# Splitting the picks' dot products between VectorE and ScalarE in a two-block transformer kernel

## The chip, the cores and the metric

The kernel runs on one core of a Trainium2 chip. The core has TensorE (PE in the rows), VectorE (DVE), ScalarE (ACT), GpSimd (POOL) and SyncE (SP), each with its own queue that runs strictly in the order in which it was written, and 16 DMA engines that all queues share. Engines wait for each other through semaphores. The metric is device time in microseconds (us); the times of before are the median of 3 runs. Everything is float32.

## The reference, cut to what matters

Two blocks follow each other on 256 tokens of width 1024. The first one ends in a retrieval of single-neuron experts (PEER), and that is where the change lies. For each token and each of 8 heads it scores two times 128 keys, takes the 16 best of each, combines them into 256 candidates, and takes the 16 best of those: the picks. Each pick names one of 16384 rows of two tables:

```python
top_s, pos = lax.top_k(combo, PEER_TOPK)
expert = jnp.take_along_axis(ids, pos, axis=-1)
g = jax.nn.softmax(top_s, axis=-1).astype(hb.dtype)
u_sel = peer_u[expert]
a = jax.nn.gelu(jnp.einsum('bqhkd,bqd->bqhk', u_sel, hb))
v_sel = peer_v[expert]
return jnp.einsum('bqhk,bqhkd->bqd', g * a, v_sel)
```

The second block (two layers of windowed attention and gated mixing, with large projections) starts when the sum over all picks is done.

## The kernel before

The tokens are two tiles of 128, one token to a partition. Eight heads and two tiles make 16 rounds g = 0 to 15, called heads here; each has 16 picks, so there are 256 picks. One pick is one gather: for each of 128 tokens a row of `peer_uv`, 1024 numbers of u and 1024 of v, 1 MB in all. It lands in one of 12 slots (`pair(n)`, n modulo 12; the slots lie in the tiles `rows` and `low_pairs`).

All engines work in program order, written out by hand. Within a head the picks go in four groups of four (`groups_of`), called groups 0 to 3; the last head has groups of 4, 2, 2 and then eight of one.

- **GpSimd** issues the gathers (L908 in the profile, the call that starts at L908). For pick n it waits until TensorE has summed pick n - 12 (`pair_used`).
- **VectorE** does `dot` for each pick of a group: one fused multiply and sum, 1024 wide, of the u half with the token's vector `h2_tok` in PSUM (L2070; the accumulator is read by a second short instruction). Then `weigh` makes four weights (L2081), for which it waits for the GELU. Behind the groups 0, 1 and 2 of head g it does one step each of the routing of head g + 2: `route_halves`, `route_pairs`, `route_experts` (L2020 to L2057).
- **ScalarE** waits for the group's four dots (`dotted`), takes their GELU (L1146), waits for `weighted` and writes four diagonal matrices (L1152). Up to head 4 its queue holds two more things: between groups 1 and 2 `score_query` copies the next queries out of PSUM as soon as TensorE has made them (L1109), and between groups 2 and 3 `score_out` copies the key scores (L1115). At a head's end stands `gate_exps`, an exponential with its table load (L1129), behind which the table for GELU is loaded again.
- **TensorE** multiplies a pick's v half by its diagonal and adds into PSUM (`sum_pair`, L1576), eight matmuls a pick, each of which is two in the rows, so a group is x64. Up to head 4 `score_query` of head g + 3 (L1552) stands between groups 1 and 2 and `score_keys` (L1565) between groups 2 and 3.

The queries and scores of the last heads are thus made while the first five heads (0 to 4) are summed; from head 5 on the picks are alone but for small things (a transpose, `join`, two weight pieces of the next block). SyncE loads one 1 MB weight unit during the picks.

Of the kernel before, what the change touches and what calls it, by code (L numbers as in the profile page):

```python
# [14 lines left out]
ALU = mybir.AluOpType  # L15
ACT = mybir.ActivationFunctionType
# [8 lines left out]
NT = T // P  # L25
D = 1024
# [6 lines left out]
EXPERT_HEADS, KEYS, PICKS = 8, 128, 16  # L33
# [220 lines left out]
def groups_of(g):  # L254

    sizes = [GROUP] * (PICKS // GROUP)
    if g == NT * EXPERT_HEADS - 1:
        sizes = [GROUP, 2, 2] + [1] * SINGLES
    at, out = 0, []
    for size in sizes:  # L260
        out.append((at, size))
        at += size
    return out
# [6 lines left out]
LAST_GROUP = NT * EXPERT_HEADS - 1  # L270
# [47 lines left out]
def build(nc, a, out):  # L318
    ctx = ExitStack()
    with ctx:  # L320
# [3 lines left out]
        def sem(name):  # L324
            return ctx.enter_context(nc.semaphore(name))
# [103 lines left out]
        dots = [w3.take(PICKS) for _ in range(2)]  # L429
# [13 lines left out]
        def pair(n):  # L443

            k = n % SLOTS
            return rows[:, k, :] if k < PAIRS else low_pairs[:, k - PAIRS, :]
# [39 lines left out]
        h2_tok = [pj[:, :, :].rearrange("p b n -> p (b n)"), aux[:, 0:2, :].rearrange("p b n -> p (b n)")]  # L486
# [38 lines left out]
        def at(l, per, k):  # L525
# [10 lines left out]
        h2_turned = sem("h2_turned")  # L536
        routed, gate_exp, dotted, dots_act, weighted, diag_ready = (
            sem("routed"), sem("gate_exp"), sem("dotted"), sem("dots_act"), sem("weighted"), sem("diag_ready"))
        pair_loaded = [sem(f"pair_loaded{s}") for s in range(SLOTS)]
        pair_used = sem("pair_used")  # L540
        single_gates, single_diag = sem("single_gates"), sem("single_diag")
# [387 lines left out]
        def _(act):  # L929
# [212 lines left out]
            for g in range(NT * EXPERT_HEADS):  # L1142
                for k, (first, size) in enumerate(groups_of(g)):
                    some = slice(first, first + size)
                    act.wait_ge(dotted, g * PICKS + first + size)
                    nc.scalar.activation(act_dots[g % 2][:, some], dots[g % 2][:, some], ACT.Gelu_apprx_tanh).then_inc(dots_act, 1)  # L1146
                    if size > 1:
                        act.wait_ge(weighted, GROUPS_BEFORE[g] + k + 1)
                    for j in range(first, first + size if size > 1 else first):
                        if g:  # L1150
                            act.wait_ge(pair_used, (g - 1) * PICKS + j + 1)
                        nc.scalar.activation(diag[:, j, :], ident[:, :], ACT.Copy, scale=weight[g % 2][:, j:j + 1]).then_inc(diag_ready, 1)  # L1152
                    h = g + AHEAD + 1
                    if h < EXPERT_HEADS and k == 1:
                        score_query(h)
                    if h < EXPERT_HEADS and k == 2:
                        score_out(h)
                    if g == EARLY_GROUP and k < EARLY_PIECES:
                        layer_hi(act, 0, k)
                    if g == LAST_GROUP and first == 11:  # L1160
                        act.wait_ge(pair_used, XH_PICKS)
                        x0_hi(0)
                if g + AHEAD < NT * EXPERT_HEADS:
                    gate_exps(g + AHEAD)
# [592 lines left out]
        def _(dve):  # L1757
            v = nc.vector
# [306 lines left out]
            def dot(g, j):  # L2065

                n = g * PICKS + j
                dve.wait_ge(pair_loaded[n % SLOTS], 16 * (n // SLOTS + 1))
                row = pair(n)[:, 0:D]
                v.tensor_tensor_reduce(row, row, h2_tok[g // EXPERT_HEADS], 1.0, 0.0, ALU.mult, ALU.add,  # L2070
                                       dots[g % 2][:, j:j + 1]).then_inc(dotted, 1)

            def weigh(g, k, first, size):

                some = slice(first, first + size)
                dve.wait_ge(dots_act, GROUPS_BEFORE[g] + k + 1)
                if size == 1:
                    v.tensor_scalar(diag[:, first, :], ident[:, :], act_dots[g % 2][:, some], weight[g % 2][:, some], ALU.mult, ALU.mult) \
                        .then_inc(single_diag, 1)
                    return  # L2080
                v.scalar_tensor_tensor(weight[g % 2][:, some], act_dots[g % 2][:, some], gate_inv[g % EXPERTS], gate[g % EXPERTS][:, some],  # L2081
                                       ALU.mult, ALU.mult).then_inc(weighted, 1)
# [17 lines left out]
            for g in range(NT * EXPERT_HEADS):  # L2100
                t, nxt = g // EXPERT_HEADS, g + AHEAD
                if g % EXPERT_HEADS == 0:
                    dve.wait_ge(h2_turned, t + 1)
                dve.wait_ge(gate_exp, g + 1)
                chain.link(v.reciprocal(gate_inv[g % EXPERTS], gate_sum[g % EXPERTS]))
                for k, (first, size) in enumerate(groups_of(g)):
                    for j in range(first, first + size):
                        dot(g, j)
                    weigh(g, k, first, size)
                    if g == LAST_GROUP and first + size == PICKS - SINGLES:  # L2110
                        singles = slice(first + size, PICKS)
                        v.tensor_scalar(weight[g % 2][:, singles], gate[g % EXPERTS][:, singles], gate_inv[g % EXPERTS], None, ALU.mult) \
                            .then_inc(single_gates, 1)
                        dve.wait_ge(single_gates, 1)
                        dve.wait_ge(pair_used, (g - 1) * PICKS + PICKS)
                    if nxt < NT * EXPERT_HEADS:
                        if k == 0:
                            route_halves(nxt)
                        if k == 1:
                            route_pairs(nxt)  # L2120
                        if k == 2:
                            route_experts(nxt)
                    if g == EARLY_GROUP and k == 3:
                        layer_lo(dve, 0, *range(EARLY_PIECES))
                    if g == EARLY_GROUP + 1:
                        dve.wait_ge(bias_iota, 1)
                        for h in (2 * k, 2 * k + 1):
                            v.tensor_scalar(bias8[:, h, :], distance, -(2.0 ** -(h + 1)) / ATT_SCALE, None, ALU.mult).then_inc(bias_lin, 1)
                    if g == LAST_GROUP and first == 12:
                        dve.wait_ge(pair_used, XL_PICKS)  # L2130
                        x0_low(0)
                if g == EXPERT_HEADS + 1:
                    dve.wait_ge(pair_used, EXPERT_HEADS * PICKS)
                    join(0)
# [263 lines left out]
```

## Time and profile before

| | us |
|---|---|
| median of 3 runs | 1173.74 (1173.55 to 1173.74) |
| the profiled execution | 1174.32 |
| its span, first to last instruction | 1172.5 |
| TensorE busy | 1048.3 (89%) |
| VectorE busy | 838.1 (71%) |
| ScalarE busy | 429.7 (37%) |
| GpSimd busy | 269.9 (23%) |
| share of the chain of waits: PE, DMA, DVE, ACT | 62%, 25%, 7%, 4% |

Three stages can be told apart. Up to about 190 us the first block's projections and attention run. From 178 us (the first gather) to 833 us (the last dot) the picks are gathered, scored and summed. Behind that the second block runs to the end. The busy shares are means over all three and say little of any one of them; the windows of the picks have to be read on their own. A line's busy time counts the instruction alone, and the wait ahead of it is given as idle time with the engine and line that ended it.

### The profile page before, as it was taken

The numbers are of one execution on the slowest core, as the hardware profiler recorded it, in microseconds if no ns is written. First come the engines' busy times: TensorE is split into PE (matmuls) and PEld (weight loads), VectorE is DVE, ScalarE is ACT, GpSimd is POOL, SyncE is SP. The second block draws the span as 40 slices with busy tenths as digits, with TensorE's granted clock in tenths as the row PEclk, the third lists the DMA queues.
The fourth block names the chain that finished last, engine by engine and source line by source line (L and its number), as shares of the span: only waits on it lengthen the run. The fifth ranks groups of instructions, "written<-read, shape, count | busy, mean of one in ns | idle before, by whom it ended". The sixth has DMA issues, their size and how long they took to land.

```text
span 1172.5 us, 18875 instructions
## 1 busy us (share of the span) xinstructions
PE 1048.3 (89%) x7587; PEld 978.6 (83%) x7587; DVE 838.1 (71%) x1802; ACT 429.7 (37%) x905; POOL 269.9 (23%) x289
## 2 busy tenths in 40 slices
PE   7999997999999988777787778878999999999997
PEld 6999986998899887677787777778999888898885
DVE  6998987667567667666777766655665868775776
ACT  3636732123212221222132122211457554476452
POOL 2001004343334333333333333434000000300000
PEclk9999998999999999999899999989999999999999
DMA  9986858999999999999999999999865655455540
GB/s 370 407 329 226 349 191 330 420 421 421 420 421 420 421 420 421 420 421 421 420 421 420 420 421 422 420 421 420 340 221 176 229 202 180 158 202 180 194 165 36
DMA packets 59576, 390.35 MB, mean 333 GB/s; under 512 B 6881, under 2 KB 7905, under 8 KB 15714
## 3 DMA queue, kind: packets, MB, share of 16 engines
q0 software_dynamic: 36864, 268.45, 55.1%
q1 hardware_dynamic: 21152, 120.10, 27.6%
q8 instruction: 60, 0.98, 0.3%
q10 hardware_dynamic: 1474, 0.60, 0.2%
q14 instruction: 26, 0.21, 0.0%
HBM read 388.08 MB, written 1.05 MB: 332 GB/s over the span
## 4 chain that ended last, share of the span: by engine, by line
PE 62%; DMA 25%; DVE 7%; ACT 4%; issue 1%; SPq 0%; ACTq 0%; DVEq 0%
PE aux L1576 23%; DMA rows<-in_peer_uv,work 23%; PE pj L1619 6%; PE pj L1620 6%; PE pj L1621 6%; PE pj L1293 5%; PE pj L1295 5%; PE pj L1294 5%; PE aux L1552 4%; DVE rows L2070 2%; DVE rows L1767 1%; DMA rows<-in_w_ada 1%; ACT work L1152 1%; ACT rows L1019 1%; PE aux L1432 1%
## 5 line engine op out<-in xcount | busy, mean ns | idle before, releaser
L1576 PE MATMUL aux<-work,rows 128*128 128x128 f32 x2080 | 261.0, 289 | 73.7 <-ACT work L1152 73.7
L1576 PEld LDWEIGHTS aux<-work,rows 128*128 128x128 f32 x2080 | 253.8, 204 | 81.4 <-ACT work L1152 81.0
L1576 PE MATMUL aux<-work,low_pairs 128*128 128x128 f32 x2016 | 237.7, 279 | 31.0 <-ACT work L1152 31.0
L1576 PEld LDWEIGHTS aux<-work,low_pairs 128*128 128x128 f32 x2016 | 232.8, 195 | 34.5 <-ACT work L1152 34.5
L908 POOL DMA_INDIRECT rows<-in_peer_uv,work x130 | 122.8, 945 | 297.8 <-PE aux L1576 230.3
L715 DVE TENSOR_TENSOR wlo<-wring,whi 128x1024 fp32r<-128x1024 f32 x98 | 118.5, 1235 | 76.8 <-ACT whi L709 76.3
L908 POOL DMA_INDIRECT low_pairs<-in_peer_uv,work x126 | 118.7, 942 | 158.9 <-PE aux L1576 154.2
L1293 PE MATMUL pj<-xh,whi 128*128 128x256 f32 x512 | 146.9, 287 | 0.3 <-DVE wlo L647 0.2
L1146 ACT ACTIVATE work<-work 128x4 f32<-128x4 f32 (+2 forms) x71 | 14.7, 207 | 359.0 <-DVE work L2070 359.0
L1295 PE MATMUL pj<-xh,wlo 128*128 128x256 f32 x512 | 145.4, 284 | 0.0
L1294 PE MATMUL pj<-xl,whi 128*128 128x256 f32 x512 | 145.4, 284 | 0.0
L2070 DVE CUSTOM_DVE_ANT_0 low_pairs<-low_pairs,aux 128x1024 f32<-128x1024 f32 x64 | 77.6, 1220 | 53.5 <-DMA low_pairs<-in_peer_uv,work 53.3
L709 ACT CAST whi<-wring 128x1024 fp32r<-128x1024 f32 x98 | 100.2, 1050 | 24.0 <-PE pj L1621 23.5
L2070 DVE CUSTOM_DVE_ANT_0 rows<-rows,aux 128x1024 f32<-128x1024 f32 x64 | 77.0, 1218 | 38.1 <-DMA rows<-in_peer_uv,work 38.0
L1293 PEld LDWEIGHTS pj<-xh,whi 128*128 128x128 f32 x512 | 98.9, 193 | 2.4 <-issue 1.8
L1294 PEld LDWEIGHTS pj<-xl,whi 128*128 128x128 f32 x512 | 98.8, 193 | 0.0
L1295 PEld LDWEIGHTS pj<-xh,wlo 128*128 128x128 f32 x512 | 98.7, 193 | 0.0
L2070 DVE CUSTOM_DVE_ANT_0 rows<-rows,pj 128x1024 f32<-128x1024 f32 x66 | 78.1, 1217 | 16.9 <-DMA rows<-in_peer_uv,work 16.6
L2070 DVE CUSTOM_DVE_ANT_0 low_pairs<-low_pairs,pj 128x1024 f32<-128x1024 f32 x62 | 73.6, 1217 | 19.9 <-DMA low_pairs<-in_peer_uv,work 19.8
L1152 ACT ACTIVATE work<-ident,work 128x128 f32<-128x128 f32 x248 | 79.4, 390 | 18.8 <-DVE work L2081 18.8
L1619 PE MATMUL pj<-whi,xh 128*128 128x512 f32 x184 | 72.6, 395 | 0.0
L1621 PE MATMUL pj<-wlo,xh 128*128 128x512 f32 x184 | 71.7, 390 | 0.0
(290 smaller groups left out, 1475.6 us busy)
## 6 DMA issues: line engine op xcount, KB each, us to landing
wring<-in_w SPq DMA_DIRECT2D x76, 1024.0 KB, 4.9
rows<-in_w_ada SPq DMA_DIRECT2D x46, 512.0 KB, 9.2
rows<-in_w SPq DMA_DIRECT2D x3, 1024.0 KB, 11.2
rows<-in_peer_uv,work POOLq DMA_INDIRECT x130, 17.3
work<-in_late_rows SPq DMA_DIRECT2D x2, 1024.0 KB, 8.5
xT<-in_gate_rows SPq DMA_DIRECT2D x2, 1024.0 KB, 7.0
rows<-in_norm_rows SPq DMA_DIRECT2D x2, 1024.0 KB, 7.2
low_pairs<-in_peer_uv,work POOLq DMA_INDIRECT x126, 18.1
```

The costliest lines, as they stand in the source:

```text
L709: nc.scalar.copy(layer_part("hi", l, p), layer_raw(l, p)).then_inc(w_hi, 1)
L715: dve.tensor_tensor(layer_part("lo", l, p), layer_raw(l, p), full(layer_part("hi", l, p)), ALU.subtract).then_inc(w_lo["d"], 1)
L908: pool.indirect_dma_start(out=pair(n), out_offset=None, in_=a["peer_uv"], in_offset=bass.IndirectOffsetOnAxis(ap=expert[g % EXPERTS][:, j: ...
L1152: nc.scalar.activation(diag[:, j, :], ident[:, :], ACT.Copy, scale=weight[g % 2][:, j:j + 1]).then_inc(diag_ready, 1)
L1293: mm(o, w[0], x[0], start=start, stop=False, skip_group_check=skip)
L1294: mm(o, w[0], x[1], start=False, stop=False, skip_group_check=skip)
L1295: return mm(o, w[1], x[0], start=False, stop=stop, skip_group_check=skip)
L1576: ins = mm(peer_sum[t][:, c * P:(c + 1) * P], pair(n)[:, D + c * P:D + (c + 1) * P], diag[:, n % PICKS, :], start=(n % (EXPERT_HEADS * PIC ...
L1619: mm(bank(u), hi[:, k, ts], w_hi_[:, j, :], start=(k == 0), stop=False)
L1620: mm(bank(u), lo[:, k, ts], w_hi_[:, j, :], start=False, stop=False)
L1621: ins = mm(bank(u), hi[:, k, ts], w_lo_[:, j, :], start=False, stop=(k == last))
L2070: v.tensor_tensor_reduce(row, row, h2_tok[g // EXPERT_HEADS], 1.0, 0.0, ALU.mult, ALU.add, dots[g % 2][:, j:j + 1]).then_inc(dotted, 1)
```

## The change

For heads 0 to 14 VectorE no longer sums: `dot` is a plain product in place (`tensor_tensor`, semaphore `multiplied`), and ScalarE reads each product with a Copy activation that also sums it into `dots` (semaphore `dotted`, now counted by ScalarE itself), in its own queue right ahead of the group's GELU. While there is a head to route (g up to 13) `weigh` stands behind the group's routing step and no longer ahead of it. The last head keeps the fused form under the name `last_dotted`. The number of weights, diagonals, gathers and matmuls stays.

```diff
                 for k, (first, size) in enumerate(groups_of(g)):
                     some = slice(first, first + size)
-                    act.wait_ge(dotted, g * PICKS + first + size)
+                    if g < LAST_GROUP:
+                        for j in range(first, first + size):
+                            n = g * PICKS + j
+                            act.wait_ge(multiplied, n + 1)
+                            nc.scalar.activation(pair(n)[:, 0:D], pair(n)[:, 0:D], ACT.Copy, accum_out=dots[g % 2][:, j:j + 1]).then_inc(dotted, 1)
+                        act.wait_ge(dotted, g * PICKS + first + size)
+                    else:
+                        act.wait_ge(last_dotted, first + size)
                     nc.scalar.activation(act_dots[g % 2][:, some], dots[g % 2][:, some], ACT.Gelu_apprx_tanh).then_inc(dots_act, 1)
...
                 row = pair(n)[:, 0:D]
-                v.tensor_tensor_reduce(row, row, h2_tok[g // EXPERT_HEADS], 1.0, 0.0, ALU.mult, ALU.add,
-                                       dots[g % 2][:, j:j + 1]).then_inc(dotted, 1)
+                if g < LAST_GROUP:
+                    v.tensor_tensor(row, row, h2_tok[g // EXPERT_HEADS], ALU.mult).then_inc(multiplied, 1)
+                else:
+                    v.tensor_tensor_reduce(row, row, h2_tok[g // EXPERT_HEADS], 1.0, 0.0, ALU.mult, ALU.add,
+                                           dots[g % 2][:, j:j + 1]).then_inc(last_dotted, 1)
...
                     for j in range(first, first + size):
                         dot(g, j)
-                    weigh(g, k, first, size)
+                    if nxt >= NT * EXPERT_HEADS:
+                        weigh(g, k, first, size)
...
                         if k == 2:
                             route_experts(nxt)
+                        weigh(g, k, first, size)
```

Lines of the changed kernel bear numbers up to 13 higher. First the queue of ScalarE in head 1, from the copies of the queries behind group 1 to group 3, as it stands before (`pq` holds queries, `aux` is PSUM, `work` holds dots, weights and diagonals):

```order
L1109 COPY pq<-aux 128x256 [waits expert_scores,queries] x2
L1146 ACTIVATE work<-work 128x4 [waits dotted]
L1152 ACTIVATE work<-ident,work 128x128 [waits pair_used,weighted]
L1152 ACTIVATE work<-ident,work 128x128 [waits pair_used] x3
L1115 COPY work<-aux 128x2x256 [waits expert_scores]
L1146 ACTIVATE work<-work 128x4 [waits dotted]
L1152 ACTIVATE work<-ident,work 128x128 [waits pair_used,weighted]
```

The same piece of ScalarE's queue in the changed kernel:

```order
L1110 COPY pq<-aux 128x256 [waits expert_scores,queries] x2
L1150 ACTIVATE rows,work<-rows 128x1024 [waits multiplied] x4
L1154 ACTIVATE work<-work 128x4 [waits dotted]
L1160 ACTIVATE work<-ident,work 128x128 [waits pair_used,weighted]
L1160 ACTIVATE work<-ident,work 128x128 [waits pair_used] x3
L1116 COPY work<-aux 128x2x256 [waits expert_scores]
L1150 ACTIVATE rows,work<-rows 128x1024 [waits multiplied] x2
L1150 ACTIVATE low_pairs,work<-low_pairs 128x1024 [waits multiplied] x2
L1154 ACTIVATE work<-work 128x4 [waits dotted]
L1160 ACTIVATE work<-ident,work 128x128 [waits pair_used,weighted]
```

Four 1024-wide activations stand ahead of each GELU, and for the groups 2 and 3 they stand behind the copies of the queries and of the scores, which wait for TensorE. At the turn from head 0 to group 0 of head 1 ScalarE's queue reads, before:

```order
L1129 ACT_TABLE_LOAD
L1129 ACTIVATE work<-work 128x16 [waits routed]
L1146 ACT_TABLE_LOAD
L1146 ACTIVATE work<-work 128x4 [waits dotted]
L1152 ACTIVATE work<-ident,work 128x128 [waits pair_used,weighted]
L1152 ACTIVATE work<-ident,work 128x128 [waits pair_used] x3
```

The same turn of the heads in the changed kernel, still ScalarE:

```order
L1130 ACT_TABLE_LOAD
L1130 ACTIVATE work<-work 128x16 [waits routed]
L1150 ACTIVATE rows,work<-rows 128x1024 [waits multiplied] x2
L1150 ACTIVATE low_pairs,work<-low_pairs 128x1024 [waits multiplied] x2
L1154 ACT_TABLE_LOAD
L1154 ACTIVATE work<-work 128x4 [waits dotted]
L1160 ACTIVATE work<-ident,work 128x128 [waits pair_used,weighted]
L1160 ACTIVATE work<-ident,work 128x128 [waits pair_used] x3
```

The table for GELU is loaded behind the four sums instead of ahead of the wait for the dots. On VectorE, group 2 of a head and the step `route_experts`, before (ISA is the fused multiply and sum, `pj` the PSUM that holds the tokens' vectors):

```order
L2070 ISA low_pairs,work<-low_pairs,pj 128x1024 [waits pair_loaded10]
L2070 ISA work 128x1
L2070 ISA low_pairs,work<-low_pairs,pj 128x1024 [waits pair_loaded11]
L2070 ISA work 128x1
L2081 SCALAR_TENSOR_TENSOR work<-work 128x4 [waits dots_act]
L2048 TENSOR_SCALAR work<-work 128x16
L2049 TENSOR_SCALAR work<-work 128x16
L2051 TENSOR_TENSOR work<-count,work 128x512 [waits dve_chain]
L2053 TENSOR_TENSOR work<-work 128x512 [waits dve_chain]
L2054 TENSOR_REDUCE work<-work 128x32 [waits dve_chain]
L2057 SCALAR_TENSOR_TENSOR work<-work 128x16 [waits dve_chain]
L2070 ISA rows,work<-rows,pj 128x1024 [waits pair_loaded0]
```

The same piece of VectorE's queue in the changed kernel:

```order
L2079 TENSOR_TENSOR low_pairs<-low_pairs,pj 128x1024 [waits pair_loaded10]
L2079 TENSOR_TENSOR low_pairs<-low_pairs,pj 128x1024 [waits pair_loaded11]
L2056 TENSOR_SCALAR work<-work 128x16
L2057 TENSOR_SCALAR work<-work 128x16
L2059 TENSOR_TENSOR work<-count,work 128x512 [waits dve_chain]
L2061 TENSOR_TENSOR work<-work 128x512 [waits dve_chain]
L2062 TENSOR_REDUCE work<-work 128x32 [waits dve_chain]
L2065 SCALAR_TENSOR_TENSOR work<-work 128x16 [waits dve_chain]
L2092 SCALAR_TENSOR_TENSOR work<-work 128x4 [waits dots_act]
L2079 TENSOR_TENSOR rows<-rows,pj 128x1024 [waits pair_loaded0]
```

The row that waits for `dots_act` has moved from the front of the routing step to behind it, and the next group's products stay behind it.

## Rows read from the trace of the kernel before

The timeline's columns: start in us, length in us, engine, line, operation, tiles, shapes, count, and in brackets the idle time ahead and what ended it.

**Rows 1.** windows of three stretches: busy time by engine, granted clock, DMA
```profile
...
core 0: us, PE busy (x) PEld busy (x) DVE busy (x) ACT busy (x) POOL busy (x), PEclk, DMA share, GB/s
200.00:400.00 200.00, 184.30 (x1452) 177.47 (x1453) 135.93 (x346) 50.20 (x135) 72.29 (x77) 0.98 1.01 421
400.00:800.00 400.00, 317.41 (x2584) 309.98 (x2583) 273.83 (x675) 88.00 (x238) 151.33 (x162) 0.95 1.01 421
850.00:1170.00 320.00, 314.66 (x1887) 274.71 (x1885) 225.12 (x329) 175.27 (x273) 11.57 (x4) 1.00 0.50 177
```

**Rows 2.** the chain that ended last: start, length, engine, tile, line
```profile
...
276.94 21.70 PE aux L1576 x192
298.64 6.92 PE aux L1552 x32
306.81 7.41 PE aux L1576 x64
...
386.13 7.43 PE aux L1576 x64
...
410.07 1.22 DVE rows L2070
```

**Rows 3.** the timeline, ScalarE (ACT): groups 0 to 3 of head 2
```profile
...
276.48 1.28 ACT L1152 ACTIVATE work<-ident,work 128x128 f32<-128x128 f32 x4 [0.29 <-DVE work L2081]
...
277.78 1.28 ACT L1129 ACT_TABLE_LOAD   x1
...
279.29 0.19 ACT L1129 ACTIVATION_READ_ACCUMULATOR work<-work 128x1 f32 x1
...
305.59 0.37 ACT L1109 COPY pq<-aux 128x256 f32<-128x256 f32 x1 [3.08 <-PE aux L1552]
305.86 0.21 ACT L1146 ACTIVATE work<-work 128x4 f32<-128x4 f32 x1
...
306.36 1.28 ACT L1152 ACTIVATE work<-ident,work 128x128 f32<-128x128 f32 x4 [0.29 <-DVE work L2081]
...
315.15 0.59 ACT L1115 COPY work<-aux 128x512 f32<-128x512 f32 x1 [7.52 <-PE aux L1565]
```

**Rows 4.** the same timeline, VectorE (DVE): routing steps between pick groups
```profile
...
281.62 0.48 DVE L2020 MAX8 work<-work 128x8 f32<-128x128 f32 x2
...
284.09 1.22 DVE L2070 CUSTOM_DVE_ANT_0 rows<-rows,pj 128x1024 f32<-128x1024 f32 x1
...
289.15 0.42 DVE L2038 TENSOR_TENSOR work<-work 128x256 f32<-128x256 f32 x1
...
292.05 1.21 DVE L2070 CUSTOM_DVE_ANT_0 rows<-rows,pj 128x1024 f32<-128x1024 f32 x1
```

**Rows 5.** timeline of ScalarE ahead of the picks: wide copies, accumulator read
```profile
...
112.75 2.94 ACT L640 CAST whi<-wring 128x1024 fp32r<-128x1024 f32 x3
115.59 0.60 ACT L1019 ACTIVATE rows<-rows,smax,inv_q 128x256 f32<-128x256 f32 x1
116.10 0.19 ACT L1019 ACTIVATION_READ_ACCUMULATOR rows<-rows,smax,inv_q 128x1 f32 x1
116.19 0.59 ACT L1019 ACTIVATE rows<-rows,smax,inv_q 128x256 f32<-128x256 f32 x1
```

**Rows 6.** timeline of VectorE behind the picks: two plain wide operations
```profile
...
835.42 2.36 DVE L715 TENSOR_TENSOR wlo<-wring,whi 128x1024 fp32r<-128x1024 f32 x2 [0.58 <-ACT whi L709]
```

**Rows 7.** the gathers' line L908: time from issue to landing
```profile
...
DMA to landing us min/median/max: 6.4/17.7/20.9
```

**Rows 8.** the timeline of GpSimd (POOL): the gather of pick 89
```profile
...
398.23 0.94 POOL L908 DMA_INDIRECT rows<-in_peer_uv,work  x1 [3.48 <-PE aux L1576]
```

**Rows 9.** timeline of TensorE (PE): three starts of pick sums after idle time
```profile
...
202.01 13.74 PE L1576 MATMUL aux<-work,rows 128*128 128x128 f32 x96 [5.92 <-ACT work L1152]
...
492.44 7.41 PE L1576 MATMUL aux<-work,low_pairs 128*128 128x128 f32 x64 [3.21 <-ACT work L1152]
...
623.47 9.04 PE L1576 MATMUL aux<-work,rows 128*128 128x128 f32 x64 [3.47 <-ACT work L1152]
```

More of the change, by code:

```diff
@@ L538, in build @@
             sem("routed"), sem("gate_exp"), sem("dotted"), sem("dots_act"), sem("weighted"), sem("diag_ready"))
+        multiplied, last_dotted = sem("multiplied"), sem("last_dotted")
         pair_loaded = [sem(f"pair_loaded{s}") for s in range(SLOTS)]
```

## The prediction

> **What bounds the kernel now.** Read the windows first [rows 1]. In the picks the DMA engines move 421 GB/s in both stretches at a share of 1.01. A pick is 1.0486 MB, so 421 GB/s is one pick in 2.49 us, and a head of 16 picks in 39.85 us. Behind 850 us it is TensorE that is full: 314.66 of 320 us. VectorE is full in neither of them, 135.93 of 200 and 273.83 of 400 us in the picks. So its relief by itself buys nothing.
>
> The second view is the chain of waits [rows 2], and there the picks fall in two halves. From 410.07 us on its steps start at dots that waited for a landing: the gathers alone set the pace. In the first five heads, however, the chain runs through TensorE almost without a gap: 21.70 us for twelve picks (1.81 us each), 6.92 for the queries, 7.41 for four picks, the key scores, then the next 21.70. The period, from one group 2 to that of two heads later, is (386.13 - 306.81) / 2 = 39.66 us, the same as the 39.85 of the gathers. Both are full at once. Whatever is added to TensorE's round there is lost as soon as the lead of the gathers is used up.
>
> In that round the only gaps hang on ScalarE [rows 3]. It copies the last queries at 305.59 us, has waited for TensorE until then, and starts the GELU of group 2 at once, at 305.86, and the first diagonal at 306.36. TensorE starts the group at 306.81 [rows 2], 1.25 us after it had ended the queries. The same happens behind the copy of the scores at 315.15, which waited 7.52 us. In these two places the dots were done long before.
>
> **The change part by part.** *VectorE's product.* The fused operation starts every 1.14 us; two plain ones of the same width take 2.36 us together, so they start every 1.14 us too [rows 6]. I book nothing as gained.
>
> *ScalarE's sum.* No row has a 1024-wide activation that also sums. Three 1024-wide casts and then the next instruction take 115.59 - 112.75 = 2.84 us, 0.95 each, and the accumulator read delays the next activation by 116.19 - 116.10 = 0.09 us [rows 5]. So 1.04 us each, 4.15 for a group, and some 0.15 until the last read has ended: 4.3 us. If the read of 0.19 us didn't overlap it would be 4.7; below the cast's 3.8 I see no reason to go.
>
> *Group 2 of heads 0 to 4.* The four sums stand behind the query copies, and these wait for TensorE. So at 305.86 the sums start, and not the GELU, though their products have been ready for long. Everything behind is 4.3 us later: GELU, weights, diagonals, TensorE. VectorE now does `route_experts` meanwhile, so the weights don't wait for it. TensorE idles for all of it: **+4.3 us**.
>
> *Group 3 of heads 0 to 4.* The same again behind the copy of the scores, which can't come earlier since TensorE makes the scores behind group 2: **+4.3 us**. VectorE makes the four products in 4.6 us from the weights of group 2 on, under TensorE's 7.41 us.
>
> *Group 0.* Start at 276.48 us, when ScalarE begins the diagonals of the group before, and TensorE begins 0.45 later. ScalarE is through with the exponential at 279.29 + 0.1 = 279.4 [rows 3]; four sums bring it to 283.55; the table load, before hidden ahead of the wait, takes 1.28 us from there on, to 284.9; the GELU, the weights (VectorE has ended its products and `route_halves` by 283.6, which takes 284.09 - 281.62 = 2.5 us [rows 4]) and the diagonal bring TensorE in at 285.9. It has ended the group before at 276.94 + 7.23 = 284.2, so it idles 1.7 us. *Group 1.* VectorE starts its products behind these weights at 285.3, ends at 289.95, does `route_pairs` in 292.05 - 289.15 = 2.9 us [rows 4], and TensorE starts at 293.55, 0.4 after it is through with group 0. Together **+2.1 us**.
>
> A round of heads 0 to 4 is thus 2.1 + 4.3 + 4.3 = 10.7 us longer. Head 0 begins with TensorE idle until 202.01 us [rows 9] and I put the same on it. Five heads: 5 x 10.7 = **+53.5 us** until TensorE starts group 3 of head 4.
>
> *What the gathers give back.* Pick 89 goes into the slot that the first pick of that group frees, and is issued at 398.23 us now [rows 8], then at 398.23 + 53.5 = 451.7. Until then the DMA engines have run dry, since TensorE, with 5.6 us of idle time twice and the queries' 6.92 in a round, frees slots in bursts and at a lower rate than they can fill. So it lands in the shortest time seen, 6.4 us, and not in the 17.7 of the median [rows 7]: at 458.1. Now it lands 2.49 us behind pick 88, whose dot waited for its landing until 410.07 [rows 2]: at 412.6. The shift of the landings is 458.1 - 412.6 = 45.5 us, 8 less than TensorE's: **-8 us**. From there on the gathers are back to back and nothing can be caught up.
>
> *The clock.* TensorE's picks after an idle stretch sometimes run slow at first: four picks take 7.41 us after 3.21 us of idle time, but 9.04 after 3.47, and six take 13.74 instead of some 11.1 after 5.92 us [rows 9]; the granted clock of these windows is 0.95 and 0.98 [rows 1], so part of the time is spent at 1.2 and not at 2.4 GHz. The change makes two gaps of 1.3 + 4.3 = 5.6 us in each of five heads. I take one slow start of 1.6 us a head, **+8 us**; the bounds are none and 2.6 us at each of the ten, 26.
>
> *Heads 5 to 13.* The weights come behind the routing step, 2.5 to 2.9 us later, group 3's 1.2 us later by the last sum. These hide in the 17.7 us that a gather is under way in the median, of which 6.4 is enough: over 11 us of room. The bound is nothing to a few us. Head 14 has no routing and pays 1.2 us in the same room. The last head and the second block stay as they are.
>
> The sum is 53.5 - 8 + 8 = +53.5 us on the profiled execution of 1174.32: 1227.8. The median of the runs was 0.58 below it: **1227 us**.
>
> *A rule of the notes.* The Trainium skill, "ScalarE: Activation LUTs", section "What ACT_TABLE_LOAD costs", gives a switch of the table set as about 2.66 us, of which 1.38 us is a drain. The rows here show 1.28 us for the load and the next instruction right behind it [rows 3]. That page would make group 0 some 1.4 us later in each of the five heads, 7 us in all and 1234 us; the same page, section "Rules for kernel authors", advises to keep multiplies and adds on VectorE.
>
> **The rivals.** *A, the gathers hide it.* If the lead of the gathers took up the sums, as in the later heads, the time would stay within 2 us of 1174. For it speaks the share of 1.01 in both stretches; against it that the debt of 10.7 us returns five times while the room is some 11 us once. It also comes true if ScalarE's sums were done before it blocks, which the order of its queue forbids. *B, faster.* A plain product may be quicker than the fused one here, though both start every 1.14 us in the rows. At half the cost, 0.57 us less each, it would shorten VectorE's part of the round, but the gathers are full and let nothing of that through, except ahead of TensorE's first start at 202.01 us, where four dots stand on the way: 4 x 0.57 = 2.3 us, and only if A holds as well: 1171. Below some 0.5 us less each it decides nothing. *C, the later heads starve as well.* Were the room in the ring used up in heads 5 to 13, each of 36 groups would add up to 2.9 us: up to 100 us more, some 1300. Against it stand the 11 us. *D, ScalarE's table switch costs more than 1.28 us* once real work stands ahead of it: 1.4 us in five heads, 1234 us; only the instruction behind a switch that now comes on the path can show it.
>
> **How the numbers follow.** The forecast 0.82 (D is in its range with 0.05 of that), A 0.09, B 0.02, C 0.07. Unknown costs of the forecast: no slow starts, -8; all ten, +18; sums at 4.7 for 4.3, +4; a bit more given back, -3. The range is 1210 to 1248, which leaves out A, B, most of C and the slowest starts. About 0.2% (2.3 us) is what a measurement of this kernel can tell from no change. Faster by more 0.02, within 0.08, slower 0.90.
>
> **What would show it.** Right: TensorE's round in heads 1 to 4 is 50 to 54 us and no longer 39.66; its idle time ahead of the groups 2 and 3 there is some 5.6 us where it was 1.3; the windows of 200 to 450 us show a DMA rate of about 330 GB/s, and 421 behind; ScalarE has a line with 240 activations of about 1.05 us; gathers in the first heads land in 7 us and not in 18. From the last gather to the end the time is the same. Wrong: the DMA rate stays 421 from 225 us on (A); TensorE's gaps in heads 5 to 13 grow beyond the 2.5 to 3 us that the later weights give and the rate falls there (C); a sum takes much less or more than 1.04 us; or the chain of waits in the first heads goes through VectorE.

## The result and the profile after

The changed kernel takes **1232.5 us** in the median (1230.6 to 1233.1, 4 runs) against 1173.7 for the kernel before: a ratio of **1.0494** with an interval of [1.0481, 1.0506] (the two medians by themselves give 1.0501). It is 58.8 us slower; 1227 was predicted. The profiled execution has a span of 1230.0 us, 57.5 more than before.

Look at the windows of the changed kernel first, with the columns of [rows 1]:

```profile
200.00:400.00 200.00, 158.09 (x1120) 152.58 (x1120) 100.31 (x196) 96.39 (x212) 56.78 (x60) 0.88 0.83 331
400.00:450.00 50.00, 39.03 (x272) 37.84 (x273) 26.54 (x53) 26.80 (x59) 13.11 (x14) 0.86 0.81 320
...
500.00:550.00 50.00, 38.66 (x301) 37.90 (x302) 35.01 (x76) 33.82 (x71) 17.23 (x19) 0.90 1.01 421
...
600.00:800.00 200.00, 160.21 (x1281) 156.71 (x1281) 141.58 (x281) 135.24 (x282) 75.91 (x82) 0.92 1.01 420
```

The damage is all in the first heads: up to 450 us the DMA rate is 331 and 320 GB/s where it was 421, and from 500 us on it is 421 again. No engine is full between 200 and 450 us; TensorE is busy for 158 of 200 us at a granted clock of 0.88.

The chain of waits (start, length, what) from group 2 of head 1 to group 3 of head 2, which before ran through TensorE alone [rows 2]:

```profile
279.00 4.17 ACT rows L1150 x8
284.14 8.84 PE aux L1584 x64
...
299.64 24.00 PE aux L1584 x192
323.64 6.92 PE aux L1560 x32
336.10 10.11 PE aux L1584 x64
347.72 4.17 ACT low_pairs L1150 x8
352.86 24.55 PE aux L1584 x192
...
539.91 18.69 DMA rows<-in_peer_uv,work
```

L1150 is the new sum; "x8" are four activations and their four accumulator reads. Twice in each of the first five heads four of them now stand between two pieces of TensorE's work. TensorE's round, from one group 3 to the next, is 352.86 - 299.64 = 53.22 us here. Group 3 of heads 0 to 4 starts at 247.21, 299.64, 352.86, 405.42 and 458.66 us, so the mean round is 211.45 / 4 = **52.86 us**, against 39.66 before.

ScalarE's timeline from group 3 of head 1 to group 2 of head 2 (start, duration, line, operation, the wait ahead in brackets), to be held against [rows 3]:

```profile
293.91 0.58 ACT L1116 COPY work<-aux 128x512 f32<-128x512 f32 x1 [8.95 <-PE aux L1573]
294.39 1.06 ACT L1150 ACTIVATE rows<-rows 128x1024 f32<-128x1024 f32 x1
295.35 0.19 ACT L1150 ACTIVATION_READ_ACCUMULATOR rows<-rows 128x1 f32 x1
295.44 1.04 ACT L1150 ACTIVATE rows<-rows 128x1024 f32<-128x1024 f32 x1
...
298.69 0.21 ACT L1154 ACTIVATE work<-work 128x4 f32<-128x4 f32 x1
...
305.21 1.04 ACT L1150 ACTIVATE low_pairs<-low_pairs 128x1024 f32<-128x1024 f32 x1
306.15 0.19 ACT L1150 ACTIVATION_READ_ACCUMULATOR low_pairs<-low_pairs 128x1 f32 x1
306.36 1.28 ACT L1154 ACT_TABLE_LOAD   x1
307.65 0.21 ACT L1154 ACTIVATE work<-work 128x4 f32<-128x4 f32 x1
...
330.58 0.37 ACT L1110 COPY pq<-aux 128x256 f32<-128x256 f32 x1 [3.08 <-PE aux L1560]
330.85 1.06 ACT L1150 ACTIVATE rows<-rows 128x1024 f32<-128x1024 f32 x1
...
335.14 0.21 ACT L1154 ACTIVATE work<-work 128x4 f32<-128x4 f32 x1
```

This is the mechanism. ScalarE stands for 8.95 us at the copy of the scores, with four finished products in memory behind it, and begins to sum them only when TensorE has nothing left to do. (VectorE's timeline has the four products end at 288.17 us.) The sums start every 1.04 us, and the GELU comes 298.69 - 294.39 = 4.30 us later than it could have. TensorE's timeline shows both gaps, of group 3 and of group 2:

```profile
299.64 6.01 PE L1584 MATMUL aux<-work,rows 128*128 128x128 f32 x32 [5.77 <-ACT work L1160]
...
336.10 6.54 PE L1584 MATMUL aux<-work,rows 128*128 128x128 f32 x32 [5.55 <-ACT work L1160]
```

The same two starts in the kernel before:

```profile
276.94 3.84 PE L1576 MATMUL aux<-work,rows 128*128 128x128 f32 x32 [1.48 <-ACT work L1152]
...
306.81 3.84 PE L1576 MATMUL aux<-work,rows 128*128 128x128 f32 x32 [1.26 <-ACT work L1152]
```

The gaps were 1.48 and 1.26 us, so each is 4.29 longer. The durations beside them are the second effect: two picks, x32, took 3.84 us, and take 6.0 to 6.5 here.

The new groups on the page (busy time, mean ns of one, idle time before and its releaser):

```profile
L1150 ACT ACTIVATE low_pairs<-low_pairs 128x1024 f32<-128x1024 f32 x120 | 126.1, 1052 | 60.6 <-DVE low_pairs L2079 60.5
...
L1150 ACT ACTIVATE rows<-rows 128x1024 f32<-128x1024 f32 x120 | 125.9, 1050 | 30.7 <-DVE rows L2079 30.6
...
L2079 DVE TENSOR_TENSOR low_pairs<-low_pairs,aux 128x1024 f32<-128x1024 f32 x58 | 70.1, 1219 | 47.2 <-DMA low_pairs<-in_peer_uv,work 47.1
```

ScalarE has 252 us of sums to do, and VectorE has not become faster: its plain product takes 1.22 us, as the fused one did.

Where the heads pass from one pace to the other, GpSimd issues the pick of [rows 8] here:

```profile
462.72 0.94 POOL L909 DMA_INDIRECT rows<-in_peer_uv,work  x1 [9.50 <-PE aux L1584]
```

On VectorE's timeline, the first product that waits for a landing again, and the last dot of all:

```profile
485.53 1.22 DVE L2079 TENSOR_TENSOR low_pairs<-low_pairs,pj 128x1024 f32<-128x1024 f32 x1 [1.25 <-DMA low_pairs<-in_peer_uv,work]
...
890.74 1.22 DVE L2081 CUSTOM_DVE_ANT_0 rows<-rows,aux 128x1024 f32<-128x1024 f32 x1 [1.81 <-DMA rows<-in_peer_uv,work]
```

And the landings of all gathers, to be held against [rows 7]:

```profile
DMA to landing us min/median/max: 5.3/15.1/21.2
```

Counted pick by pick, the product at 485.53 is that of the 95th pick, whose dot was at 427.45 before: 58.08 us later. The last dot was at 832.99 and is 57.75 us later. The gathers land sooner than before, in 15.1 us in the median where it was 17.7. Those issued between 250 and 450 us, in the first heads, land in 9.3 us in the median where it was 15.1: sooner, as predicted, though not in the 7 us that the prediction named. What the first five heads cost is carried through the other eleven without loss or gain, and the second block adds nothing.

### The profile page after: what moved, and what is told of

Its sections match the earlier page's. It is cut to its first block, busy times and chain, and to the rows that moved or that the text cites. A ratio compares the mean times of both kernels' runs of the same rounds, so it can differ in the third digit from the quotient of the medians.

```text
span 1230.0 us, 19115 instructions
## 1 busy us (share of the span) xinstructions
PE 1072.8 (87%) x7587; PEld 1002.9 (82%) x7587; DVE 833.0 (68%) x1562; ACT 692.8 (56%) x1385; POOL 270.5 (22%) x289
## 3 DMA queue, kind: packets, MB, share of 16 engines
q0 software_dynamic: 36864, 268.45, 53.5%
## 4 chain that ended last, share of the span: by engine, by line
PE 64%; DMA 19%; ACT 9%; DVE 6%; issue 2%; SPq 0%; POOL 0%; DVEq 0%; POOLq 0%
PE aux L1584 25%; DMA low_pairs<-in_peer_uv,work 10%; DMA rows<-in_peer_uv,work 8%; PE pj L1627 5%; PE pj L1628 5%; PE pj L1629 5%; PE pj L1301 5%; PE pj L1302 4%; PE pj L1303 4%; PE aux L1560 4%; ACT rows L1150 3%; ACT low_pairs L1150 2%; PE aux L1375 1%; DMA wring<-in_w 1%; ACT work L1160 1%
## 5 line engine op out<-in xcount | busy, mean ns | idle before, releaser
L1584 PE MATMUL aux<-work,rows 128*128 128x128 f32 x2080 | 277.0, 300 | 96.9 <-ACT work L1160 96.7
L1584 PEld LDWEIGHTS aux<-work,rows 128*128 128x128 f32 x2080 | 270.3, 215 | 103.8 <-ACT work L1160 102.9
L1584 PEld LDWEIGHTS aux<-work,low_pairs 128*128 128x128 f32 x2016 | 242.2, 202 | 45.7 <-ACT work L1160 45.4
L1150 ACT ACTIVATE low_pairs<-low_pairs 128x1024 f32<-128x1024 f32 x120 | 126.1, 1052 | 60.6 <-DVE low_pairs L2079 60.5
L1150 ACT ACTIVATE rows<-rows 128x1024 f32<-128x1024 f32 x120 | 125.9, 1050 | 30.7 <-DVE rows L2079 30.6
L2092 DVE SCALAR_TENSOR_TENSOR work<-work 128x4 f32<-128x4 f32 (+1 forms) x63 | 15.2, 242 | 152.7 <-ACT work L1154 152.7
L2079 DVE TENSOR_TENSOR low_pairs<-low_pairs,aux 128x1024 f32<-128x1024 f32 x58 | 70.1, 1219 | 47.2 <-DMA low_pairs<-in_peer_uv,work 47.1
L2079 DVE TENSOR_TENSOR low_pairs<-low_pairs,pj 128x1024 f32<-128x1024 f32 x62 | 73.1, 1215 | 17.4 <-DMA low_pairs<-in_peer_uv,work 17.2
L2079 DVE TENSOR_TENSOR rows<-rows,pj 128x1024 f32<-128x1024 f32 x66 | 77.3, 1215 | 9.8 <-DMA rows<-in_peer_uv,work 9.6
L2079 DVE TENSOR_TENSOR rows<-rows,aux 128x1024 f32<-128x1024 f32 x54 | 64.7, 1217 | 24.0 <-DMA rows<-in_peer_uv,work 23.9
```

The costliest lines, as they stand in the source:

```text
L1150: nc.scalar.activation(pair(n)[:, 0:D], pair(n)[:, 0:D], ACT.Copy, accum_out=dots[g % 2][:, j:j + 1]).then_inc(dotted, 1)
L1584: ins = mm(peer_sum[t][:, c * P:(c + 1) * P], pair(n)[:, D + c * P:D + (c + 1) * P], diag[:, n % PICKS, :], start=(n % (EXPERT_HEADS * PIC ...
L2079: v.tensor_tensor(row, row, h2_tok[g // EXPERT_HEADS], ALU.mult).then_inc(multiplied, 1)
```

## The experiments

The theory: ScalarE's queue is in order, and four sums of 4.3 us stand behind each of two copies that wait for TensorE; this lengthens TensorE's round in the five heads in which that round is as long as the gathers', and nothing elsewhere. The rivals: the later heads pay as well; the moved weights, not the sums, are what costs; the price is ScalarE's work as such and not its place; the clock.

**Only the first five heads, and only the later ones.** The change is made for g below 5 in one kernel and for g from 5 to 14 in the other (`5 <= g < 15`), and the semaphores are counted to match. The edit in `dot`:

```diff
-                if g < LAST_GROUP:
+                if 0 <= g < 5:
                     v.tensor_tensor(row, row, h2_tok[g // EXPERT_HEADS], ALU.mult).then_inc(multiplied, 1)
```

> The whole change, but for heads 0 to 4 alone; from head 5 on the fused dot and the weights' old place. If the time is lost in ScalarE's queue behind the copies of queries and scores, which stand in heads 0 to 4 only, all of it is here: 1230 to 1233 us. If the later heads pay (rival C), it is well below, 1200 or less.

> The whole change for heads 5 to 14 alone; heads 0 to 4 as before. If the gathers' time under way hides what is added there: 1173 to 1176 us, and a DMA rate of 421 GB/s throughout. By rival C most of the 59 us are here: 1200 to 1232.

Measured: the early half alone 1235.3 us (1.0516 [1.0499, 1.0534]), the late half alone 1172.5 us (0.9989 [0.998, 0.9999]), 0.5 below the range expected. All of the loss is in five of fifteen heads. The early half is even 2.8 us above the whole change, and above what was expected; its first sum of picks starts 3.5 us later than the whole change's, for a reason that the last experiments take up.

**One part of the change without the other.** In the third kernel ScalarE sums, but `weigh` stays in its old place ahead of the routing step; in the fourth the dots stay fused on VectorE and only `weigh` moves behind the routing step.

```diff
 # sums only: weigh again ahead of the routing step
-                    if nxt >= NT * EXPERT_HEADS:
-                        weigh(g, k, first, size)
+                    weigh(g, k, first, size)
...
                             route_experts(nxt)
-                        weigh(g, k, first, size)
```

> Products on VectorE and sums on ScalarE as in the change, but the weights in their old place ahead of the routing step. By the theory the sums alone cost the time: 1230 to 1236 us, since the weights wait for ScalarE in either place and group 1's products now start behind the routing. If the place of the weights is what costs, some 1180.

> The fused dot stays on VectorE, and only the weights are moved behind the routing step. By the theory 0.5 to 1 us a round in heads 0 to 4, which the gathers' room takes up: 1173 to 1177 us. If the place of the weights costs the time, 1215 or more.

Measured: sums only 1240.6 us (1.0563 [1.0545, 1.058]), weights only 1174.4 us (1.0001 [0.9991, 1.001]). The weights are not what costs. Moving them helps the sums: with the weights in the old place the round is 54.47 us and not 52.86. VectorE's timeline of the third kernel shows how, at group 0 of head 2:

```profile
314.31 0.23 DVE L2092 SCALAR_TENSOR_TENSOR work<-work 128x4 f32<-128x4 f32 x1 [4.03 <-ACT work L1154]
...
316.92 4.62 DVE L2079 TENSOR_TENSOR rows<-rows,pj 128x1024 f32<-128x1024 f32 x4
```

VectorE stands for 4.03 us until ScalarE's sums and the GELU are done, and only then routes, so the next products start 2.6 us behind these weights; in the whole change the routing fills that wait, and they start 0.14 us behind them. Moved by themselves, the weights cost a little, a round of 40.33 for 39.66 us, and the gathers hide that. The third kernel missed its expectation of 1230 to 1236 to the high side: the 1.61 us that each round is longer had not been booked, nor had a halt of 3.3 us that the last experiments take up.

**The sums ahead of the copies.** This leaves every instruction as it is and changes only where ScalarE does the sums of groups 2 and 3 in the first heads: before it blocks on the copy, not behind it. It was made for both places of the weights.

```diff
                     if g < LAST_GROUP:
-                        for j in range(first, first + size):
...
+                        if not (g + AHEAD + 1 < EXPERT_HEADS and k >= 2):
+                            row_sums(g, first, size)
...
                     h = g + AHEAD + 1
+                    if h < EXPERT_HEADS and k in (1, 2):
+                        row_sums(g, first + size, GROUP)
                     if h < EXPERT_HEADS and k == 1:
                         score_query(h)
```

> The change, with one thing moved in heads 0 to 4: ScalarE makes the sums of group 2 ahead of its copies of the queries and the sums of group 3 ahead of its copy of the scores, so that only the GELU stands behind them as before. If the order in ScalarE's queue is the cause, both gaps of TensorE fall from 5.6 to 1.3 us and only the 2.1 us of groups 0 and 1 stay, most of which the gathers take up: 1174 to 1180 us. If the sums cost by their mere work on ScalarE or by traffic, the time stays near 1232.

> As the run before, with the weights back ahead of the routing step. The theory gives nearly the same, 1174 to 1181 us; the difference of the two is what the place of the weights is worth once the sums are out of the way, expected at most 3 us either way.

Measured: 1184.7 us (1.0086 [1.0069, 1.0103]) and 1188.8 us (1.0126 [1.0109, 1.0143]). ScalarE does 240 sums as before, and five sixths of the loss are gone in the first, three quarters in the second: it is the place in the queue that costs, not the work. ScalarE's timeline of the first of them (from its second run, below), with the sums at L1137:

```profile
301.56 1.06 ACT L1137 ACTIVATE low_pairs<-low_pairs 128x1024 f32<-128x1024 f32 x1
302.52 0.19 ACT L1137 ACTIVATION_READ_ACCUMULATOR low_pairs<-low_pairs 128x1 f32 x1
308.39 0.37 ACT L1110 COPY pq<-aux 128x256 f32<-128x256 f32 x1 [5.69 <-PE aux L1567]
311.85 0.37 ACT L1110 COPY pq<-aux 128x256 f32<-128x256 f32 x1 [3.08 <-PE aux L1567]
312.11 0.21 ACT L1159 ACTIVATE work<-work 128x4 f32<-128x4 f32 x1
```

TensorE's timeline of the same run, groups 3, 0 and 2:

```profile
280.91 3.84 PE L1591 MATMUL aux<-work,rows 128*128 128x128 f32 x32 [1.48 <-ACT work L1165]
...
289.94 7.41 PE L1591 MATMUL aux<-work,low_pairs 128*128 128x128 f32 x64 [1.62 <-ACT work L1165]
...
313.07 3.84 PE L1591 MATMUL aux<-work,rows 128*128 128x128 f32 x32 [1.26 <-ACT work L1165]
```

The sums fill time in which ScalarE waited, the GELU again follows the copy at once, and the gaps are 1.48 and 1.26 us as before, with TensorE at full pace behind them (3.84 us). What is left is the 1.62 us ahead of group 0, which the prediction had as 1.7, and some 0.5 us at group 1: a round of 41.94 us, 2.28 longer than before and 2.1 above the 39.85 of the gathers. With the weights in the old place the round is 43.00 us, since TensorE also waits 1.26 us ahead of group 1, by the order of VectorE's queue shown above. Both kernels missed their expectation, by 5 and 8 us, and their difference of 4.2 us is more than the 3 expected. The last experiments give 4.8 and 4.0 us of the miss to a halt; the rest of the second's goes with the 1.06 us that each of its rounds is longer.

**Half a sum.** ScalarE sums only the first 512 of the 1024 products, so half of each dot is left out; everything else is the changed kernel.

```diff
-nc.scalar.activation(pair(n)[:, 0:D], pair(n)[:, 0:D], ACT.Copy, accum_out=...)
+nc.scalar.activation(pair(n)[:, 0:D // 2], pair(n)[:, 0:D // 2], ACT.Copy, accum_out=...)
```

> The change, with ScalarE summing only the first 512 of each 1024 products (half of the sum is left out). A sum gets 0.41 us shorter, four in a row 1.65 us, twice a round, five rounds: 16.5 us less than the change, 1216 us (1213 to 1219). If the sums are not in a row with TensorE the time stays at 1232; if more than these ten waits hang on them it falls by more than 20.

Measured: 1210.8 us (1.0311 [1.0293, 1.0328]). The gaps fell by 1.7 us each, as half of four sums should (TensorE's timeline, groups 3 and 2):

```profile
295.28 5.47 PE L1584 MATMUL aux<-work,rows 128*128 128x128 f32 x32 [4.06 <-ACT work L1160]
...
329.37 5.47 PE L1584 MATMUL aux<-work,rows 128*128 128x128 f32 x32 [3.85 <-ACT work L1160]
```

The round fell by 4.85 us, to 48.01, more than the 3.4 of the two gaps. The rest is group 0 and the slow starts: x32 takes 5.47 us here where it took 6.01 and 6.54. The expectation, 1213 to 1219 us, had booked the gaps alone and was missed to the low side.

**TensorE kept busy in the gaps.** Ten matmuls on constants, whose results nobody reads, are put behind the queries and ten behind the key scores, 4.48 us for each ten; the wait for ScalarE stays as long as it was, but TensorE does something in them.

```diff
                         score_query(h)
+                        pe.wait_ge(scores_out, h - 1)
+                        keep_busy(10, h % 2)
                     ...
                         score_keys(h)
+                        pe.wait_ge(scores_out, h)
+                        keep_busy(10, (h + 1) % 2)
```

> The change, with ten idle matmuls on TensorE (some 4.3 us) behind the queries and ten behind the scores in heads 0 to 4, into PSUM that nobody reads, so that it is at work while it waits for ScalarE. They fit into the two gaps of 5.6 us. If the slow starts behind these gaps cost what the rows show (2.5 us at group 2, 2.2 at group 3, less 1.7 of idle time ahead of group 0 that comes back), some 3 us a round: 1217 us (1213 to 1221), with groups 2 and 3 starting at full pace. If the slow starts cost nothing on the way to the end, 1232.

Measured: 1223.9 us (1.0422 [1.0405, 1.044]). TensorE's timeline, with the added matmuls as L1350:

```profile
295.17 1.06 PE L1573 MATMUL aux<-low_pairs,pq 128*128 128x128 f32 x8
296.06 4.48 PE L1350 MATMUL aux<-wsT,ident 128*128 128x256 f32 x20
301.99 3.84 PE L1584 MATMUL aux<-work,rows 128*128 128x128 f32 x32 [1.45 <-ACT work L1160]
...
332.74 4.48 PE L1350 MATMUL aux<-wsT,ident 128*128 128x256 f32 x20
338.45 3.84 PE L1584 MATMUL aux<-work,rows 128*128 128x128 f32 x32 [1.24 <-ACT work L1160]
```

Its window of 200 to 400 us:

```profile
200.00:400.00 200.00, 178.00 (x1275) 166.97 (x1275) 101.43 (x207) 104.10 (x228) 57.12 (x60) 0.97 0.85 335
```

The picks behind start at full pace, 3.84 us, and the granted clock is 0.97 and not 0.88. The round is 50.54 us: without slow starts a round is 10.88 us longer than before (10.7 had been worked out), and the slow starts make the other 52.86 - 50.54 = **2.32 us a round**. The time is above the 1213 to 1221 us expected, by a halt of 4.1 us that comes next.

**What was left over: a halt before the picks.** Several kernels so far that were paced by TensorE had come out higher than their rounds explain. The rows show where. At about 195 us, between the last queries of head 2 and their key scores, TensorE's queue stands still, and the profile names nothing that it waited for. In the kernel with the sums ahead of the copies, ScalarE's copy of the last queries and TensorE's key scores behind it:

```profile
199.86 0.37 ACT L1110 COPY pq<-aux 128x256 f32<-128x256 f32 x1 [7.87 <-remote]
...
200.34 2.05 PE L1580 MATMUL aux<-low_pairs,pq 128*128 128x128 f32 x8 [5.29 <-issue]
```

ScalarE's wait for these queries is 3.08 us in the profiled executions before and after the change, but 4.9 to 6.4 us in the four kernels of the first set, which shared a chip, and 7.1 to 7.9 in the four of the second set, on another. To see whether it belongs to the kernels, the changed kernel and the one with the sums ahead were run again on a third chip, together with the late half, whose gain was in doubt, and a variant of it with the weights in the old place (`weigh` ahead of the routing step, `5 <= g < 15` otherwise).

> The changed kernel as it is, run again, to see whether the halt of TensorE's queue at about 195 us belongs to a kernel or to an execution. If it belongs to the kernel: first sum of the picks again at 202 us, last query copy ahead of it again 3.1 us behind its predecessor, the time 1231 to 1233 us. If it belongs to the execution: the first sum between 202 and 208 us, and the time up to 4 us more.

> ScalarE's sums ahead of its copies in the first heads, run again. If the halt belongs to the kernel: it is there again, last query copy behind 7.9 us of waiting, first pick sum at about 209.8 us, time 1184 to 1187 us. If it belongs to the execution: less, and the time down to 1180 us.

> The change in the heads from 5 on only, again, in more rounds. Its ratio was 0.9989 with an interval that nearly touched 1. If the gain is real, the ratio is again 0.998 to 0.9995 and the last dot of the picks ends some 2 us earlier than before. If it was the chip's scatter, the ratio is 0.9995 to 1.001.

> The change in the heads from 5 on, but with the weights in their old place, ahead of the routing step. If the moved weights gave the gain of the late heads, this one is at the time of the kernel before (0.9995 to 1.001); if the split of the dot gave it, it is as fast as with the moved weights (0.998 to 0.9995). In any case the gathers pace these heads, so the time stays within 1171 to 1176 us.

Measured: the changed kernel 1233.0 us (1.0501 [1.0481, 1.052]) with rounds of 52.88 us and its first sum of picks at 203.3 us; the sums ahead of the copies **1179.9 us** (1.0048 [1.003, 1.0066]), 4.8 less than the same kernel on the other chip; the late half 1173.0 us (0.9991 [0.9982, 1.0]) and its variant 1173.3 us (0.9994 [0.9985, 1.0003]). The same two rows of the same kernel here:

```profile
193.89 0.37 ACT L1110 COPY pq<-aux 128x256 f32<-128x256 f32 x1 [3.08 <-PE aux L1567]
...
194.36 1.13 PE L1580 MATMUL aux<-low_pairs,pq 128*128 128x128 f32 x8 [0.51 <-issue]
```

No halt in any of the four. Two of the kernels, the sums ahead and the late half, were profiled on a chip with the halt and on the one without, so it goes with the chip, or with something else that was the same within a set of runs, and not with the kernel. Where TensorE sets the pace it falls on the time; where the gathers do, it is hidden: the late half halted 1.8 us in its first run and not in its second, and took 1172.5 and 1173.0 us. The kernel before has 1174.1, 1174.4 and 1174.2 us in the three sets; whether it halted in the first two isn't known, since it was profiled in none of them. So, if a halt adds its whole length, the times of the first two sets above the kernel before are too high by up to their halt: 2.6 us (early half), 3.3 (sums only), 4.8 and 4.0 (sums ahead), 4.0 (half a sum), 4.1 (kept busy). Taken off, the early half is at 1232.8 us, the whole change's time, and the others stand at some 1237, 1180, 1185, 1207 and 1220. For the sums ahead of the copies the third chip shows just that, 1179.9; for the others these are estimates, each from the halt of one profiled execution.

The late half has come out ahead of the kernel before in both sets, by 1.6 and 1.2 us. Its windows show the gathers at full rate, so the split of the dot neither helps nor harms there:

```profile
200.00:400.00 200.00, 186.26 (x1473) 179.24 (x1473) 136.60 (x351) 51.68 (x138) 73.51 (x79) 0.99 1.01 420
450.00:800.00 350.00, 284.52 (x2262) 278.94 (x2261) 235.93 (x445) 230.08 (x483) 134.58 (x143) 0.92 1.01 421
```

From the first gather to the last dot it takes 831.21 - 177.50 = 653.71 us, against 832.99 - 178.29 = 654.70 before. A gain of 0.1%, with an interval that touches 1 in the second set, is less than the bound named in the prediction, and it isn't claimed; whether the moved weights or the split would give it stays open.

## Why the prediction was right, and where its terms were off

**What bounds the kernel.** The reading of [rows 1] and [rows 2] that both TensorE's round and the gathers are full in the first five heads, and the gathers alone behind, is what the two halves show: +61 us (58.7 without the halt) for five heads, nothing for ten.

**VectorE's product**: booked at no gain, and 1.22 us each, as the fused one. **ScalarE's sum**: 1.04 us each and 4.3 us for four, from three casts and one accumulator read [rows 5]; the rows of after show 1.04 and 4.30.

**Groups 2 and 3**: +4.3 us each; measured 5.55 - 1.26 and 5.77 - 1.48, both 4.29. Moving the sums ahead of the copies took exactly these away. **Groups 0 and 1**: +2.1 us. With TensorE kept busy the queries follow 325.83 - 301.99 = 23.84 us behind the start of group 3, and in the kernel before they followed 21.54 us behind it (298.48 - 276.94 on TensorE's timeline): +2.30. In the changed kernel it is 323.47 - 299.64 = 23.83: there the slow start of group 3 runs in the time that TensorE would otherwise wait ahead of group 0, and costs nothing in this round.

**The round**: 10.7 worked out, 10.88 measured without slow starts, which is 4.29 + 4.29 + 2.30. From group 3 of head 0 to that of head 4 the change is 211.45 - 158.63 = 52.82 us, for which 4 x 10.7 and four slow starts of 1.6 us, 49.2, had been booked. Head 0 was booked like the others. The shift there is 9.9 us: the first sum starts at 202.06 us as before, although its gap grew by 2.5 us, because the queries ahead of it were through 2.5 us earlier in this execution (1.2 in the second run of the kernel).

**The clock** is the term that was mis-sized. The forecast had one slow start of 1.6 us a head, 8 in all, since the rows showed slow and full starts behind nearly the same gap [rows 9]. After a gap of 5.6 to 5.8 us every start was slow: groups 2 of heads 0 to 4 took 9.96, 8.84, 10.11, 8.88 and 10.13 us for 7.41. The forecast put 1.6 us a head on this; it is 2.32 us a round by the kernel that was kept busy, 11.6 in five, inside the bounds of 0 and 26. Nearly all of it comes from group 2: its starts in heads 1 to 4 are 2.08 us over in the mean, while those of group 3, up to 2.8 us over, add 0.25, since the wait ahead of group 0 takes them up.

**What the gathers give back**: 8 us forecast. The pick of [rows 8] is issued 64.5 us later and landings are 58.1 us later, so 6.4 come back of that. The first product that waits for a landing, six picks on, is at 485.53 us; counted back at 2.49 us each, this pick landed at 470.6, 7.9 us behind its issue and not in the 6.4 us of the shortest. Its issue also comes 1.7 us later than TensorE's shift, since the first sum of a group is slow now.

Added up against the 53.5 us of the sum: head 0 gave 9.9 us for 12.3 (-2.4), the other four rounds 52.8 for 49.2 (+3.6), the later issue +1.7 and the smaller give-back +1.6, together +4.6 and 58.1 us at the landings. The two profiled executions are 57.7 us apart and the medians 58.8, which makes most of the rest of the 5.5 by which 1227 was low.

**Heads 5 to 13 and the tail**: booked at nothing, and nothing it is. Half of a sign that the prediction named against itself did come: the gaps grew, to 3.9 and 5.0 us ahead of some groups. But the rate did not fall, it stayed 420 to 421 GB/s: they are waits for landings, not their cause.

**The rivals.** A, the gathers hide it: refuted by 331 GB/s. Its condition, ScalarE's sums done before it blocks, brings the time to 1179.9 us: near, but 5.7 us above 1174 and not within 2, by what groups 0 and 1 still add. B, faster: a plain product is no quicker. C, the later heads starve: the late half alone refutes it. D, a dearer table switch: the GELU starts at 307.65 us, 1.29 behind the start of its table load at 306.36, though four wide activations and their reads stand ahead of it. The Trainium skill, "ScalarE: Activation LUTs", section "What ACT_TABLE_LOAD costs", counts a drain of 1.38 us with a switch; no such time lies ahead of the load either (the last read ends at 306.34), so the measurement decides against it here.

## What to carry to other kernels

Before work is moved to an engine with idle time, look at what that idle time is: ScalarE was busy for a third of the span, but here it stood at the head of an in-order queue, blocked by the very engine that would next wait for the moved work. The same 240 sums cost 59 us behind two blocking copies and some 6 us ahead of them. And where two resources are full at once, as TensorE's round and the gathers were, find the stretches where that is so: the same edit was free in ten heads and cost 12 us in each of the other five.

## What the runs showed of the chip

- TensorE's start behind an idle gap costs more than the gap. Behind 5.6 us of idle time the next four picks took 1.4 to 2.8 us longer, every time; behind 1.3 to 1.6 us, in the same heads of the other kernels, they took their 7.41. With matmuls on constants in the gap, which left 1.2 to 1.5 us of it, they did so too, at a granted clock of 0.97 where it was 0.88. That gave back 8.7 us of the whole kernel, 12.7 with the halt taken off, against the 11.6 of five rounds.
- A queue can halt with nothing in the records that it waits for. At about 195 us, while the last of the first twelve gathers were being issued, TensorE stood for up to 4.8 us more on two chips and not on a third, two of the kernels being the same. What it waited for was not found, and no experiment looked for it. Comparisons against a kernel that hides it (1174.1 to 1174.4 us everywhere) overstate the loss of the others by up to that much.
- Summing beside the copy costs ScalarE 0.09 us: a start every 1.04 us for 1024 columns, against 0.95 for casts of the same width [rows 5].
